# Three-block transformer kernel on Trainium2: the mixture-of-experts stage of its first block recut from passes of 64 slots in column slabs to passes of 32 slots in row slabs

## What is computed

```python
logits = (h @ w_router) + b_router                    # 256 x 32
top_v, top_i = lax.top_k(logits, TOP_K)               # 4 of 32
gates = jax.nn.softmax(top_v, axis=-1)
...
u = xb @ w_mlp1[e] + b_mlp1[e]                        # 1024 -> 2048
x_glu = jnp.minimum(u[..., ::2], 7.0)
x_lin = jnp.clip(u[..., 1::2], -7.0, 7.0)
a = x_glu * jax.nn.sigmoid(1.702 * x_glu) * (x_lin + 1)
return a @ w_mlp2[e] + b_mlp2[e]                      # 1024 -> 1024
```

## Time and profile before

| | us |
|---|---|
| median of 3 runs (lowest, highest) | 2804.03 (2801.33, 2805.39) |
| the profiled execution | 2805.73 |
| its span on the core | 2804.1 |
| PE busy | 2324.6 (83%) |
| DVE busy | 577.4 (21%) |
| ACT busy | 397.0 (14%) |

### The profile page before, as it was taken

How to read it: one execution, slowest core, us unless ns; L and a number is a source line. 1 busy time by engine, 2 the same in 40 slices (tenths; PEclk the granted TensorE clock), 3 DMA queues, 4 the chain that set the end, 5 groups by cost and what they waited for, 6 DMA issues and landing times.

```text
span 2804.1 us, 31586 instructions
## 1 busy us (share of the span) xinstructions
PE 2324.6 (83%) x12610; PEld 1264.3 (45%) x12611; DVE 577.4 (21%) x1319; ACT 397.0 (14%) x862; POOL 98.9 (4%) x131
## 2 busy tenths in 40 slices
PE   4976598989898989899898987799979998765564
PEld 3855322223222322233235866489965546332232
DVE  1043451111111111112111075200031202120002
ACT  1142110111101011111111143100001113110001
POOL 4000000000000000000000000000000000000000
PEclk9985689999999999999999997899989999867788
DMA  9460569999999799997963474246524342289975
GB/s 289 114 241 0 192 249 369 387 373 387 373 387 382 255 385 383 376 386 279 381 229 127 150 275 147 90 150 158 151 98 135 120 129 96 67 286 324 350 259 195
DMA packets 363561, 681.86 MB, mean 243 GB/s; under 512 B 15922, under 2 KB 122675, under 8 KB 363232
## 3 DMA queue, kind: packets, MB, share of 16 engines
q1 hardware_dynamic: 325616, 535.79, 54.6%
q0 software_dynamic: 37856, 144.98, 14.3%
q10 hardware_dynamic: 16, 0.02, 0.0%
HBM read 679.70 MB, written 1.06 MB: 243 GB/s over the span
## 4 chain that ended last, share of the span: by engine, by line
PE 68%; DMA 15%; DVE 7%; SPq 6%; ACT 3%; issue 1%; DVEq 0%; ACTq 0%
PE ps L664 29%; PE ps L966 15%; DMA ring<-in_w_mlp 11%; PE ps L988 5%; DMA MOD<-in_w 3%; PE ps L1259 3%; SPq L513 2%; PE ps L970 2%; SPq L514 2%; SPq L455 2%; PE ps L729 2%; PE ps L938 2%; PE ps L997 2%; DMA ring<-in_w_ada 1%; PE ps L831 1%
## 5 line engine op out<-in xcount | busy, mean ns | idle before, releaser
L966 PE MATMUL ps<-ring,scr 128*64 128x512 f32 x1680 | 527.3, 636 | 96.7 <-DMA ring<-in_w_mlp 95.0
L966 PEld LDWEIGHTS ps<-ring,scr 128*64 128x64 f32 x1680 | 158.8, 146 | 413.9 <-issue 412.9
L664 PE MATMUL ps<-ring,HTY 128*128 128x512 f32 (+5 forms) x960 | 328.4, 503 | 3.7 <-ACT HTY L1340 3.7
L664 PE MATMUL ps<-HTY,ring 128*128 128x256 f32 (+2 forms) x1392 | 298.8, 385 | 2.4 <-ACT HTY L1340 2.4
L664 PEld LDWEIGHTS ps<-HTY,ring 128*128 128x128 f32 (+2 forms) x1392 | 247.9, 182 | 51.2 <-ACT HTY L1340 3.6
L966 PE MATMUL ps<-MOD,scr 128*64 128x512 f32 x560 | 247.8, 595 | 0.0
L988 PE MATMUL ps<-HTY,scr 128*64 128x512 f32 x560 | 246.1, 592 | 1.0 <-ACT scr L1506 1.0
L988 PE MATMUL ps<-scr 128*64 128x512 f32 x560 | 246.1, 592 | 0.0
L664 PEld LDWEIGHTS ps<-ring,HTY 128*128 128x128 f32 x960 | 175.5, 191 | 153.4 <-issue 137.3
L2113 DVE TENSOR_SCALAR scr<-ps 128x256 f32<-128x256 f32 x70 | 29.7, 425 | 864.9 <-PE ps L970 864.9
L1259 PE MATMUL ps<-ring,scr 128*32 128x512 f32 x432 | 78.8, 709 | 111.5 <-DMA MOD<-in_w 110.8
(11 more groups left out here) (416 smaller groups left out, 2152.8 us busy)
## 6 DMA issues: line engine op xcount, KB each, us to landing
ring<-in_w_mlp SPq DMA_DIRECT2D x96, 2048.0 KB
MOD<-in_w_mlp SPq DMA_DIRECT2D x32, 2048.0 KB
HTY<-in_w_mlp POOLq DMA_DIRECT2D x32, 2048.0 KB, 10.4
scr<-in_w_mlp POOLq DMA_DIRECT2D x32, 2048.0 KB, 16.6
ring<-in_w_ada SPq DMA_DIRECT2D x24, 2048.0 KB, 9.1
ring<-in_w SPq DMA_DIRECT2D x48, 1024.0 KB, 11.7
ring<-in_w_in SPq DMA_DIRECT2D x21, 2048.0 KB, 7.8
ring<-in_w_ff SPq DMA_DIRECT2D x16, 2048.0 KB, 9.0
```

The costliest lines, as they stand in the source:

```text
L664: mm = pe.matmul(o, lhs(k), rhs(k), start=begin and k == 0, stop=end and k == nk - 1)
L966: pe.matmul(ps[C1 * s:C1 * (s + 1), b, :], XG[:, k, :], m1_slabs[2 * b + s][:, k, :], start=k == 0, stop=False)
```

## The change

Passes have 32 slots (`C1 = 32`). Their grid is worked in four column strips of the array:

- **Slabs.** Slabs 0 to 3 hold 256 rows each of the up matrix (all 2048 columns: runs of 8 KB in HBM), 4 and 5 hold 512 rows each of the down matrix (runs of 4 KB). `up(n, 0)` uses slabs 0 and 1, `up(n, 1)` slabs 2 and 3 and then the bias. SP reissues slabs 0, 1 and 2 each when its own semaphore says that it was used, slab 3 and the bias row (one load in place of four) when `up` is through.
- **Products.** `up` is 8 steps over four strips with 512 columns each; the result of a pass is one bank. `down` is 4 steps over four strips (two halves of the columns by two halves of the sum, which `scatter` adds). `gather` has 256 columns in each of four strips. The activation, its transpose and the copies are done once for a pass and not twice.
- **Routing.** The best four come from a search (`max`, `match_replace`); the place products wait for the mask alone. The transpose of the gates and the product with the down bias move from ahead of pass 0 to behind its `up`. There is no list of slots and gates: DVE reads the expert's number from `work` (a register load in each pass) and takes the column from `EPLACE` and `GT`.
- **POOL** loads slab 5 of expert 0 at `mix_ready` and slab 4 after the route product; the table `c_before` is no longer loaded.

```diff
-C1 = 64
+C1 = 32
+STRIPS = 4
@@ sync
-                sp.dma_start(b1row[32 * j:32 * j + 1, :], ...
-                sp.dma_start(m1_slabs[j], kpn(I["w_mlp1"][0][e][:, cols_])).then_inc(m1_landed[j], 16)
+                sp.dma_start(m1_slabs[j], kpn(I["w_mlp1"][0][e][2 * P * j:2 * P * (j + 1), :])).then_inc(m1_landed[j], 16)
...
-                for j in range(4):
-                    sp.wait_ge(m1_up[j // 2], through)
+                for j in range(3):
+                    sp.wait_ge(m1_slab_used[j], through)
                     expert_slab(e, j)
+                sp.wait_ge(m1["up"], through)
+                expert_row(e)
+                expert_slab(e, 3)
@@ gpsimd
-                pool.dma_start(m1_slabs[j], kpn(I["w_mlp2"][0][e][:, BANK * (j - 4):BANK * (j - 3)])).then_inc(m1_landed[j], 16)
+                pool.dma_start(m1_slabs[j], kpn(I["w_mlp2"][0][e][BANK * (j - 4):BANK * (j - 3), :])).then_inc(m1_landed[j], 16)
+            pool.wait_ge(mix_ready, 1)
+            expert_slab(0, 5)
...
             pool.wait_ge(product_ready, end["route1"])
             expert_slab(0, 4)
-            pool.wait_ge(gates_ready, 1)
-            expert_slab(0, 5)
@@ tensor
-            pe.wait_ge(gates_ready, 1)
...
+            pe.wait_ge(m1["masked"], 1)
...
-                for k in range(KT):
-                    for s in range(2):
-                        pe.matmul(ps[C1 * s:C1 * (s + 1), b, :], XG[:, k, :], m1_slabs[2 * b + s][:, k, :], ...
+                    for k in (2 * j, 2 * j + 1):
+                        for t in range(STRIPS):
+                            mm = pe.matmul(ps[32 * t:32 * (t + 1), 0, :], XG[:, k, :], m1_slabs[j][:, k % 2, BANK * t:BANK * (t + 1)], ...
+                    if j < 3:
+                        mm.then_inc(m1_slab_used[j], 1)
...
+                for kk in range(4):
+                    for half in range(2):
+                        for s in range(2):
+                            t, c = divmod(4 * s + kk, 2)
+                            r = 64 * half + 32 * s
+                            mm = pe.matmul(ps[r:r + 32, 3, :], aT[:, c, C1 * t:C1 * (t + 1)],
+                                           m1_slabs[4 + s][:, kk, BANK * half:BANK * (half + 1)], start=kk == 0, stop=kk == 3)
...
+                up(n, 0, e)
+                turn_hidden(n - 1)
+                gather(n + 1)
+                down(n - 1, e_before)
+                turn_tokens(n + 1)
+                up(n, 1, e)
+                scatter(n - 1)
                 back(n)
@@ vector
+            for a in range(NT):
+                step(dve.max(TOPL[:, a, :], LOGITS1[:, a, :]))
+                step(dve.match_replace(CHOSEN1[:, a, :], TOPL[:, a, :], LOGITS1[:, a, :], -1.0e30))
+            tell(dve.tensor_tensor(MASK[:, :, :], CHOSEN1[:, :, 4:], LOGITS1[:, :, 4:], ALU.not_equal), m1["masked"], 1)
...
+            def pick(e, offset, n, astep):
+                astep(dve.tensor_copy(gcur.unsqueeze(2), GT[:, :, bass.ds(e, 1)]))
+                astep(dve.tensor_scalar(rcur.unsqueeze(2), EPLACE[:, :, bass.ds(e, 1)], offset, None, ALU.subtract))
+                picked(n)
...
-            for half in halves:
-                number = iota[:, half].unsqueeze(2).to_broadcast(shape)
-                step(dve.tensor_tensor(SEL[:, half], number, ESTART.unsqueeze(1).to_broadcast(shape), ALU.is_ge))
...
```

More of the change, by code:

```diff
@@ L285, in build @@
[L285 to L292, removed]
@@ L294, in build @@
[L294 to L295 removed]
+        XG, XS, GPT = carve(512, KT, C1), carve(768, S), carve(1024, S)
+        PICK, PICKG = carve(1280, NT, C1), carve(1344, NT, STRIPS, C1)
+        glu, lin1, sig, aS = carve(1600, 256), carve(1856, 256), carve(2112, 256), carve(2368, 256)
+        aT, YS = carve(2624, 2, P), carve(2880, BANK)
@@ L296, in build @@
+        WORK = carve(4084, END1)
+        gatesT = scr[0:E1, 4224:4480]
+        b2row = scr[0:E1, 4480:5504]
+        m1_slabs = [shaped(ring[:, j, :], (2, 2 * F1)) for j in range(3)] + [
+            MOD[:, 1:5, :].rearrange("p (k m) d -> p k (m d)", k=2), shaped(HTY[:, :], (4, D)), carve(9216, 4, D)]
         GLA_KD = carve(10496, 2, 2, S)
@@ L968, in up @@
[L968 to L975, removed]
+                    if j == 3:
+                        pe.wait_ge(m1_row_landed, 16 * e + 16)
+                    pe.wait_ge(m1_landed[j], 16 * e + 16)
+                    for k in (2 * j, 2 * j + 1):
+                        for t in range(STRIPS):
+                            mm = pe.matmul(ps[32 * t:32 * (t + 1), 0, :], XG[:, k, :], m1_slabs[j][:, k % 2, BANK * t:BANK * (t + 1)],
+                                           start=k == 0, stop=False)
@@ new lines, in up, with turn_hidden @@
+                    if j < 3:
+                        mm.then_inc(m1_slab_used[j], 1)
+                if b == 1:
+                    for t in range(STRIPS):
+                        mm = pe.matmul(ps[32 * t:32 * (t + 1), 0, :], ones[32 * t:32 * t + 1, 0:C1], b1row[32 * t:32 * t + 1, :],
+                                       start=False, stop=True)
+                    mm.then_inc(m1["up"], 1)
+            def turn_hidden(n):
+                pe.wait_ge(m1["hidden"], n + 1)
+                pe.wait_ge(m1["back_read"], n + 1)
@@ L1025, in _ @@
             turn_tokens(0)
-            expert_pass(0, 0, None)
+            pe.wait_ge(m1["gather_read"], 1)
+            up(0, 0, 0)
+            up(0, 1, 0)
+            start_sums()
+            gather(1)
+            turn_tokens(1)
+            back(0)
             pe.wait_ge(m1["listed"], 1)
@@ L2060, in _ @@
-            pick(0, step)
-            step(dve.tensor_scalar(EPASS, count, float(C1), 1.0, ALU.is_gt, ALU.add))
-            for r in range(2, -(-S // C1)):
-                step(dve.scalar_tensor_tensor(EPASS, count, float(C1 * r), EPASS, ALU.is_gt, ALU.add))
-            through = WORK[:, THROUGH:THROUGH + E1]
-            step(dve.tensor_tensor_scan(through, ones[:, 0:E1], EPASS, 0.0, ALU.mult, ALU.add))
-            step(dve.tensor_copy(WORK[:, 0:1], through[:, E1 - 1:]))
-            tell(dve.tensor_copy(work[:, 0:OF_PASS], WORK[:, 0:OF_PASS]), m1["counted"], 1)
```

278 lines of the change are left out of this document (118 added, 160 removed).

## The result

The changed kernel takes **2855.22 us** (median of four runs, 2848.08 to 2866.37) against 2802.68 for the kernel before beside it: a ratio of 1.0194 (95% interval 1.0166 to 1.0222), some 52 us slower. The forecast was 2819, so the sign and the mechanism came out and the size did not. The profiled execution took 2848.08 (span 2846.4), the fastest of the four.

A forecast was written before the change was run, and what follows sets the result against it. Loads bind one-pass experts, PE the extra passes. 364 + 20×36 + 8×33.3 + 2×48.8 + 47.5 + 2.8 + 3 = 1501 us stage end, some 15 later: median 2819; own range 2799 to 2843, wide (8 in 10) 2720 to 2862.

The forecast's parts named there:

- first `down` ends: Stage start: slabs 0 and 1 land at 355, `up(1, 0)` 5.8, transposes and `gather` 1.3, first `down` over at about 364.
- 20 one-pass experts: Experts 1 to 31 with one pass: a cycle of 36 us each, taken between bounds of 32.7 and 38.1.
- 8 two-pass experts: Two passes of 15.4 plus 2.5, 33.3 us each, down slabs loading in their own first pass with nothing beside them.
- experts 17 and 27: Experts with three passes, put at 48.8 us each.
- register loads: DVE's register load ahead of `pick(n + 1)`: 0.2 us in each of 14 extra passes, 3 in all; one-pass experts hide it.
- rival A: Engines switch in pieces of at most 4 KB, so equal shares: one-pass cycle 30.5 us, kernel 2709; chance 0.17.
- the sum's upper bound: One-pass cycle with POOL 1.1 us alone, then a third: 2.5 + 1.1 + 27.2 + 1.5 + 5.8 = 38.1 us.
- the lead: Time POOL's down slabs load alone before SP's packets come, one-pass experts: 1.1 us, none behind a two-pass expert.
- the lower bound: One-pass cycle if POOL has 3.8 us alone: 2.5 + 3.8 + 19.1 + 1.5 + 5.8 = 32.7 us.
- rival B: Down slabs get thirds but POOL's whole lead counts: one-pass cycle 32.7 us, kernel 2753, mostly faster; chance 0.22.
- The sums' start: 7.19 us on PE moved behind `up(0)`, hidden by waiting for expert 1's slabs until about 355; uncovered it costs 7.
- 26 and 60 us won against 60 lost: Stage balance: 26 won at the start, some 60 in several-pass experts and less one-pass work, lost to 20 cycles longer by 3.

The follow-up runs named there:

- e4_small: Changed kernel with the loads of experts 1 to 31 cut to an eighth of their columns (times only, no valid result); 2415.4 us, one run.
- e1: Changed kernel with each up slab loaded in two halves of its columns, runs of 4 KB and not 8; 2753.6 us, ratio 0.9830 to before.
- e8: Changed kernel with each up slab loaded in four quarters of its columns, runs of 2 KB; 2778.2 us, ratio 0.9889 to before.
- e6: Changed kernel with down slabs in 8 KB runs, cut by `down`'s steps, slab 4 reissued after the second step; 2683.4 us, ratio 0.9551 to before.
- e10: Changed kernel with down slabs cut by `down`'s steps and given back one by one, runs still 4 KB; 2726.1 us, ratio 0.9708 to before.
- e7: Changed kernel with 8 KB down runs, down slabs given back one by one, sums started behind `up(1, 1)`; 2680.6 us, ratio 0.9544 to before.
- e3_onequeue: Changed kernel with all six slabs on SP's queue, POOL issuing none; 2754.5 us, ratio 0.9814 to before.

## Why the prediction was right in kind and short in size

By its own steps, with the stage's end at 1531.07 and not 1501 (30.1 late) against 1485.3 before. The profiled execution is 27 us over its forecast of 2821; the median is 36 over 2819, as the other three executions were slower than the profiled one.

| step | predicted | measured | late by |
|---|---|---|---|
| first `down` ends | 364 | 375.7 | 11.7 |
| 20 one-pass experts | 36 | 34.4 | -32 |
| 8 two-pass experts | 33.3 | 38.7 | 43 |
| experts 17 and 27 | 48.8 | 53.3, 51.6 | 7.3 |
| expert 31, to its last `down` | 47.5 | 50.5 | 3.0 |
| register loads | 3 | in the rows above | -3 |

**Right.** The first `up` starts at 339.80 (338.6 predicted), SP's slab 0 is reissued at 343.66 (342). An unwaited pass is 15.6 us against 15.4; the difference is in `gather` and the transposes, and the register loads cost nothing there (PE is busy for 689.92 of the 690 us from 380 to 1070 in e4_small). The wait moves from SP's up slabs to POOL's down slabs for the stated reason: packets alternate one for one, so SP's 8 KB get two thirds; e1 and e8 make that three points of one law. That the engines might switch in pieces of at most 4 KB (rival A) is out. The Trainium skill ("DMA: Bandwidth & Descriptors", section "SWDGE vs HWDGE vs iDMA") has the engines round-robin between queues packet by packet; every DMA view above agrees (171 and 171, 268 and 267, 333 and 335).

**One-pass experts, 34.4 and not 36.** The mean hides levels, by what stands next to the expert. With SP ahead and POOL without a lead (the experts 1, 4, 10, 13 and 18) it is 38.7 to 39.1, where the sum's upper bound had 38.1. In a run of one-pass experts (5, 6, 7, 19, 20, 21), where 35 to 37 was the sign to look for, it is 33.5 to 34.9. There the lead is not the 1.1 us counted but close to the 3.8 of the lower bound and of rival B: SP issues slab 2 at 529.05, and from 529 to 533 us POOL has 311 packets and SP 2. What is above the 32.7 comes behind that, 21.8 us to the landing and not 20.6, and 6.3 for the slow `down` and not 5.8.

Ahead of an expert of several passes (2, 8, 11, 14, 22) it is 30.1 to 30.9, and between two such (16, 26, 28, 30) 33.2 to 34.7: there the first pass of the next expert gives no up slab back, so SP has less to load beside POOL (behind expert 1 it issues nothing from 423.44 to 457.58). That case the prediction had not seen, and no run was made for it alone. So the mean lies between the two bounds, single experts outside them on both sides, and the value taken, 36, was too high. This error of 32 us has the other sign and hid part of the next ones, which is luck.

**Two-pass experts, the step that failed.** The text had "2 × 15.4 + 2.5 = 33.3 us, as its down slabs load in its own first pass with nothing beside them". They do load alone but for the last 3 us, and yet not within the pass: 0.7 us to POOL's first issue, 0.7 to its second, 14.16 until slab 5 has landed and 0.1 for PE to see it make 15.8 from the end of one `down` to the start of the next, and the pass leaves 12. PE waits 3.7 us, and two `down`s of this cycle run at the lower clock: the one ahead, behind the wait of the one-pass expert 2, takes 6.27 us in place of 3.48, the one behind 5.34. That is 22.0 + 17.3 = 39.3 for expert 3. In the prediction's sum the 2.5 us were all that was left for this. The parts of such a round trip stood in the prediction's own one-pass sum (2.5 to the first packets, 10.2, landing 1.5) and weren't held against the pass in the two-pass one. e6 and e10 are the test: with half the round trip under the `down` they take 32.9 and 31.4. The experts 17 and 27 go the same way, from 53.3 and 51.6 to 47.0 and 47.5 in e6.

**The start, 11.7 us.** The sums' start was to move "behind `up(0)`, where PE waits for expert 1's slabs until about 355". That cover was not there: the first `up` with its bias took 10.6 us and not 8.1 and ended at 350.4 and not 346.7, the gates' copy on ACT took until 353.3, and the 7.19 us ran from there to 360.4, with `gather(1)`, two copies and a load of a register (1.80 us of issue) still behind. The text did give the price if the cover failed (7 us), and put no chance on it. e7 beside e6 shows it: 11.7 us from the first `up` to the first `down`.

**The balance in words.** The sum of the steps adds up to 1501, but the sentence behind it does not give +15: 26 and 60 us won against 60 lost would be a gain. Against the kernel before, whose first `down` ends at 406.2, whose twenty one-pass experts take 32.6 us and whose eight others 33.0, the same steps win 42 us up to the first `down` and 15 in the experts 17 and 27. They lose 68 in the twenty, 3 in the eight and 3 in the register loads: 16 us longer. The start was worth more than the 26 us, and the experts of several passes won far less than 60.

**Outside the stage** the changed kernel is 3.5 us shorter (span less the stage's end, 1315.3 against 1318.8).

So terms were mis-sized (two-pass experts 43 us, three-pass ones 10, the start 12 too low; one-pass ones 32 too high), with the mechanism as told; the forecast's own range of 2799 to 2843 missed 2855, the wide one held it.

## What to carry to other kernels

Where two DMA queues share the engines, the length of a packet is a priority: give the queue with the least slack packets at least as long as the other's, and when you lengthen one queue's runs, look at who shares with it. A buffer that is loaded only when its last use has ended puts the whole round trip (here 15.8 us for 4.19 MB) between two uses: compare it with the shortest distance between uses, also where nothing competes, and if it is longer, cut the buffer by order of use and give it back in parts. A wait costs twice on PE, by its length and by the clock of what stands behind it.

## What the runs showed of the hardware

The length of a run sets the share, also above 4 KB: packets of 8 KB on both queues give nearly equal bytes and 423 GB/s (e7_all, 550 to 555 us):

```profile
DMA packets 264, 2.11 MB, mean 423 GB/s; under 512 B 6, under 2 KB 6, under 8 KB 6
...
q0 software_dynamic: 132, 1.08, 51.8%
q1 hardware_dynamic: 132, 1.03, 49.6%
```

One queue alone is no slower (e3_onequeue, 550 to 555 us, packets of 4 and 8 KB):

```profile
DMA packets 381, 2.17 MB, mean 434 GB/s; under 512 B 16, under 2 KB 16, under 8 KB 216
```

So nothing in these traces holds a core to the 358 GB/s that the prediction took from the Trainium skill's page "DMA: Bandwidth & Descriptors" (section "Bandwidth"). The same section ties that figure to two cores streaming from one HBM domain and gives 425 GB/s for one core alone; this program runs on one core, and its traces, with 423 and 434 GB/s over 5 us, agree with the second figure.

A queue that starts beside a busy one sees its first packets late. In the changed kernel POOL's come 1.5 us after an issue with nothing beside it (527.42) and 3.9 us after one beside SP's loads (485.85); SP's come after 1.1 (343.66) and 3.8 (529.05). So the queue that starts first has the engines to itself for longer than the issues are apart.

PE's clock falls in a wait and takes part of the next work to come back. Windows of the changed kernel (last three columns: granted clock, DMA share, GB/s), PE idle from 499.5 on:

```profile
480.00:490.00 10.00, 10.00 (x98) 3.06 (x94) 0.00 (x0) 1.36 (x3) 1.48 (x2) 1.00 1.01 423
490.00:500.00 10.00, 7.41 (x60) 2.25 (x60) 2.75 (x8) 1.95 (x5) 0.00 (x0) 1.00 1.02 418
500.00:510.00 10.00, 0.00 (x0) 0.00 (x0) 0.00 (x0) 0.00 (x0) 0.00 (x0) 0.60 1.01 414
510.00:520.00 10.00, 0.00 (x0) 0.00 (x0) 0.00 (x0) 0.00 (x0) 0.00 (x0) 0.50 1.02 420
```

At 0.50 (1.2 of 2.4 GHz) the `down` at 520.24 took 6.44 us and not 3.48, and the clock was back at 1.00 from 527 on. The prediction had 2.3 us for such a wait; it is nearer 3.
